# Prompt attention: turns under the single-pass type, and low-key products of two query tiles in the array's row halves

## Chip, cores and metric

One core of one Trainium2 chip. The metric is the device time of one execution in microseconds (us), as a median of several runs; lower is better. A difference of 0.2% is about what a measurement of this kernel can tell from none.

## The reference, cut to what matters

Two layers over a prompt of 2,048 tokens and 8 running streams of 16 new tokens each, in float32: first a gated short convolution, then stick-breaking attention with 16 heads of 64. The change lies wholly in the attention of the prompt:

```python
z = jnp.einsum('bqhd,bkhd->bhqk', q, k, preferred_element_type=jnp.float32) * scale
causal = kpos[None, :] < qpos[:, None]
log_keep = jnp.where(causal, jax.nn.log_sigmoid(-z), 0.0)
rev = lax.cumsum(log_keep, axis=log_keep.ndim - 1, reverse=True)
...
a = jnp.exp(log_a)
o = jnp.einsum('bhqk,bkhd->bqhd', a, v.astype(jnp.float32))
```

So each query has a weight for each earlier key: the sigmoid of their score, times the product over all keys between them of one minus their sigmoids.

## The kernel before

The kernel runs in stages: input norm and the first layer's projections, the convolution, its output projection, the values and keys, the prompt's attention (the stage of the change), and a last stage with the samples' attention and the output projection.

**Split numbers.** A float32 operand of a product is held as a high part, rounded to the type float32r (F32R), and a low part, the rest. A product of two such operands is done as several matmuls in F32R.

**The stage's work.** For each of 16 heads (eight pairs `pr`, two heads `hh` each) the 2,048 by 2,048 scores are cut into units of 512 queries by 512 keys, and each unit into four pieces of 128 queries (`q` 0 to 3). On the diagonal the pieces are 128, 256, 384 and 512 keys wide. There are 640 pieces in all, 448 of them 512 wide. Each piece goes this way:

1. TensorE, `score`: two matmuls into a buffer `pz` in PSUM, of which there are two (`ZS`). The stationary operand is the query tile in `q2`, whose 128 rows are the 64 of the high part and the 64 of the low one. The moving operand is first `kh2` (high keys, both row halves alike), L1801, then `kl2` (low keys, both halves alike), L1802.
2. ScalarE: two sigmoids of `pz`, into `a` (L1875) and, of the negated score, into `keep` (L1876). Then `pz` is free again.
3. VectorE, `scan`: the running product of `keep` from the right, into `prod` (L1926 on the diagonal, L1932 elsewhere, where it starts from the piece four before it).
4. GpSimd, `weigh`: `a` times `prod` (L1981).
5. When a unit's pieces are weighted, TensorE, `turn`: four blocks of 128 keys are turned (transposed), each with up to four instructions of 128 by 128 (L1825, 2,176 in all), into `pt`. The tile of `a` is the stationary operand, the identity the moving one, both float32.
6. ScalarE copies the block to its high part `ath` (L1885), and VectorE takes the low part `atl` as the difference (L1942).
7. TensorE, `product`: two matmuls with the values, of `ath` (L1814) and `atl` (L1816), which add up in `po`. ScalarE copies `po` out at the end of a group (L1891).

Between these, TensorE also does 280 times two parts ("chunks") of the projections for queries and gate (L1843 to L1845), whose operands SyncE loads; ScalarE (L1898, L1901) and VectorE (L1949, L1953) take up the results.

**Order.** Each engine works through a list that the class `Line` draws up when the kernel is built. It steps through time with a cost for each item (`pe_time`, `act_time`, `dve_time`, `pool_time`, and 0.1085 us for a turn of 128 columns) and takes on each engine, among the next items of each kind that could start earliest, the one with the best rank. On the chip an engine executes its list in order and waits at semaphores. SyncE's list holds the loads: the queries and keys of a head are fetched when the scores of the head two before it are done, the chunks' operands when their buffers come free.

Of the kernel before, what the change touches and what calls it, by code (L numbers as in the profile page):

```python
# [13 lines left out]
P = 128  # L14
# [1163 lines left out]

NPAIR = H // 2

ZS, TS, US, KS, PS, AS = 2, 3, 4, 4, 8, 4

Q_PAIRS = NPAIR - 2
PARTS = 4
# [6 lines left out]
X_AT = 12 * SEQ  # L1191
X_SIZE = 2 * 2 * (KT // 2) * PW * 4
LATE_SIZE = X_AT + X_SIZE + 3 * PW * 4


def is_diagonal(u):
# [51 lines left out]

ENGINES = "PE", "ACT", "DVE", "POOL", "SP"
N_HEAD, N_OUT = 2 * NPAIR, 2 * NPAIR * NGQ  # L1250
SCORE_LEAD, CHUNKS_END, CHUNKS_FROM, CHUNK_PACE = 13, 0.96, -0.01, 6


def pe_time(w):

    return w / 2400 + 0.0155


def act_time(w):
# [20 lines left out]
class Line:  # L1280


    def __init__(self):
        self.at = {}
        self.free = dict.fromkeys(ENGINES, 0.0)
        self.lines = {e: [] for e in ENGINES}
        self.loads = []
        self.pieces = [(h, n) for h in range(N_HEAD) for n in range(N_PIECE)]
        self.blocks = [(h, b) for h in range(N_HEAD) for b in range(N_BLOCK)]
        self.outs = [(h, b) for h, b in self.blocks if ends_group(b)]  # L1290
        self.chunks = all_chunks()
        self.gates = [c for c in self.chunks if c[3] == PARTS - 1]
        self.splits = [(un, m, half) for un in range(N_UN) for m in (Q, Z) for half in range(2) if (un, m) != (0, Q)]
        self.splits.sort(key=lambda s: (s[0], s[1]))
        self.next = collections.Counter()
        self.whole = sum(2 * pe_time(piece_width(n)) for _, n in self.pieces)
        self.whole += sum((QG - block_from(b) // P) * 0.1085 + 2 * pe_time(QG * P - block_from(b))
                          for _, b in self.blocks)
        self.spent = 0.0
        for part in range(PARTS):  # L1300
            self.at["x", 0, 0, part] = X_LANDS[part]
        for half in range(2):
            self.at["split", 0, Q, half] = 0.0
        for h in range(2):
            for what in KEYS:
                self.at[what, h] = 0.0 if h == 0 else FIRST_DONE
            self.at["v_in", h] = V_LANDS if h == 0 else FIRST_DONE
        for m in (Q, Z):
            self.at["raw", 0, m] = 0.0
        self.free["SP"], self.moved = X_LANDS[0] + 10.0, FIRST_DONE  # L1310
# [97 lines left out]
    def work(self, what):  # L1408

        k = self.next[what]  # L1410
        if what in ("score", "sigmoid", "scan", "weigh"):
            w = piece_width(self.pieces[k][1])
            if what == "score":
                return 2 * pe_time(w), 0.249 + 0.000469 * w - pe_time(w)
            if what == "sigmoid":
                return 2 * act_time(w), 0.185 - 0.000036 * w
            if what == "scan":
                return 0.06 + 0.0022 * w - (0.04 if w == P * QG and is_diagonal(PIECES[self.pieces[k][1]][0]) else 0), 0.135
            return pool_time(w), 0.09
        if what in ("turn", "high", "low", "product"):  # L1420
            w = QG * P - block_from(self.blocks[k][1])
            if what == "turn":
                return 0.1085 * w / P, 0.2
            if what == "high":
                return act_time(w), 0.185 - 0.000036 * w
            if what == "low":
                return dve_time(w), 0.15
            return 2 * pe_time(w), 0.249 + 0.000469 * w - pe_time(w)
# [15 lines left out]
    def place(self, engine, what, start):  # L1444
# [18 lines left out]
        if what in ("score", "sigmoid", "scan", "weigh"):  # L1463
            h, n = self.pieces[k]
            line.append((what, *divmod(h, 2), n))
            if what == "score" and n == N_PIECE - 1:
                pr, hh = divmod(h, 2)
                if pr + 1 < NPAIR:
# [53 lines left out]
    def queries(self, h):  # L1522

        pr = h // 2 + 1
        if ("scored", h) in self.at and (pr < 2 or ("made", pr) in self.at):
            ready = max(self.at["scored", h], self.at.get(("made", pr), 0.0))
            self.move(ready, 2, ("queries", *divmod(h, 2), 0), 2, 1.05, ("queries", h + 2))

    def work_of(self, what, k):

# [64 lines left out]
def phase_attend(nc, x_d, qz_v, w_room, qh_t, ql_t, kh_t, kl_t, sz_t, v_prompt, ident, oa_t, ob_t,  # L1595
# [4 lines left out]
    with ExitStack() as ctx:  # L1600
# [2 lines left out]
        at_late = lambda n, at: late(f"a_{n}1", [P, SEQ], F32R, at)  # L1603
        q2, kh2, kl2 = ([mine, at_late(n, i * 4 * SEQ)]
                        for i, (n, mine) in enumerate((("q", early.q), ("kh", early.kh), ("kl", early.kl))))
        v2 = [at_top("a_v0", [P, QT, 2, HD], F32R, V_AT), sb("a_v1", [P, QT, 2, HD], F32R)]
        x = late("a_x", [P, PARTS, PART_KT, 2, PW], F32R, X_AT)
        raw, (wh0,), (wl0,), (_, gain) = w_room
        wh, wl = [wh0, sb("a_wh1", [P, KT, P], F32R)], [wl0, sb("a_wl1", [P, KT, P], F32R)]
        v_in = sb("a_v_in", [P, 2, QT, HD])  # L1610
        a = sb("a_a", [P, US, QG, Z_W])
        keep = sb("a_keep", [P, KS, Z_W + 1])
        prod = sb("a_prod", [P, PS, Z_W + 2])
        ath = sb("a_ath", [P, AS, QG * P], F32R)
# [8 lines left out]
        restart = pb("a_restart", [P, Z_W])  # L1623
        assert nc.sbuf_base <= early.top - (TOP_SIZE - EARLY_SIZE)
        passed, passed_sp, q_rest = sem("a_passed"), sem("a_passed_sp"), sem("a_q_rest")
        qk_loaded, v_loaded = sem2("a_qk_loaded"), sem2("a_v_loaded")
        v_hi, v_ready = sem2("a_v_hi"), sem2("a_v_ready")
        z_ready, z_used, scanned, weighted = (sem("a_" + n) for n in ("z_ready", "z_used", "scanned", "weighted"))
        t_ready, at_hi, at_split, av_done = (sem("a_" + n) for n in ("t_ready", "at_hi", "at_split", "av_done"))
        ends_set, restart_set, o_read = sem("a_ends_set"), sem("a_restart_set"), sem("a_o_read")  # L1630
        x_loaded = sem2("a_x_loaded", PARTS)
        raw_loaded = sem2("a_raw_loaded")
        w_scaled, w_hi, w_ready = ([sem(f"a_w_{n}_{m}") for m in "qz"] for n in ("scaled", "hi", "ready"))
# [25 lines left out]
        def _(sp):  # L1659
            def load(pr, hh, sources):  # L1660

                rows = bass.ds((2 * pr + hh) * HD, HD)
                for dst, top, bottom in sources:
                    for part, src in ((slice(0, HD), top), (slice(HD, P), bottom)):
                        sp.dma_start(dst[hh][part, :].bitcast(F32), src[rows, 0:SEQ]).then_inc(qk_loaded[hh], 16)

            def load_v(pr, hh):
                cols = bass.ds((2 * pr + hh) * HD, HD)
# [94 lines left out]
                    load_raw(pr + 1)  # L1763

            queries, high_keys, low_keys = ((q2, qh_t, ql_t),), ((kh2, kh_t, kh_t),), ((kl2, kl_t, kl_t),)
            sp.wait_ge(early.x_stored, 16 * 4 * KT)
            load_x(0, 0)
            last_stores(sp)
# [14 lines left out]
        def _(pe):  # L1783
# [3 lines left out]
            def score(pr, hh, n):  # L1787
# [3 lines left out]
                if is_pair(pr, 0) and hh == 0:  # L1791
                    if n == 0:
                        pe.wait_ge(early.first_loaded, 96)
                    elif g == ORDER[1] and is_diagonal(u) and q == 0:
                        pe.wait_ge(q_rest, 32)
                elif n == 0:
                    pe.wait_ge(qk_loaded[hh], 96 * (pr + hh))
                pe.wait_ge(z_used, piece(pr, hh, n - ZS) + 1 + ZS)
                o = pz[:, n % ZS, 0:w]
                lhs = q2[hh][:, i * P:(i + 1) * P]  # L1800
                pe.matmul(o, lhs, kh2[hh][:, p0:p0 + w], start=True, stop=False)  # L1801
                pe.matmul(o, lhs, kl2[hh][:, p0:p0 + w], start=False, stop=True).then_inc(z_ready, 1)  # L1802

            def multiply(pr, hh, b):
                u, j = BLOCKS[b]
# [12 lines left out]

            def turn(pr, hh, b):
                u, j = BLOCKS[b]  # L1820
                if j == 0:
                    pe.wait_ge(weighted, piece(pr, hh, QG * u + QG) + N_PIECE)
                wait_past(pe, at_split, blk(pr, hh, b) + 1 - TS)
                for q in range(block_from(b) // P, QG):
                    mm = pe.transpose(pt[:, turn_slot(pr, hh, b), q * P:(q + 1) * P],  # L1825
                                      a[:, unit_slot(hh, u), q, j * P:(j + 1) * P], ident[:, :])
                mm.then_inc(t_ready, 1)

            def chunk(pr, gx, m, part):
# [87 lines left out]
        def _(dve):  # L1917
            dve.sem_inc(scanned, N_PIECE)

            def score(pr, hh, n):  # L1920
                u, q = PIECES[n]
                w, s = piece_width(n), n % PS
                dve.wait_ge(z_used, piece(pr, hh, n) + 1 + ZS)
                dve.wait_ge(weighted, piece(pr, hh, n - PS) + 1 + N_PIECE)
                if is_diagonal(u):
                    dve.tensor_tensor_scan(prod[:, s, scan_from(n):Z_W + 1][:, ::-1], keep[:, n % KS, 0:w][:, ::-1],  # L1926
                                           restart[:, Z_W - w:Z_W][:, ::-1], 0.0,
                                           ALU.mult, ALU.add).then_inc(scanned, 1)
                else:
                    dve.wait_ge(scanned, piece(pr, hh, n - QG) + 1 + N_PIECE)  # L1930
                    before = scan_from(n - QG)
                    dve.tensor_tensor_scan(prod[:, s, 0:w + 1][:, ::-1], keep[:, n % KS, 0:w + 1][:, ::-1],  # L1932
                                           restart[:, 0:1].broadcast_to([P, w + 1]),
                                           prod[:, (n - QG) % PS, before:before + 1],
                                           ALU.mult, ALU.bypass).then_inc(scanned, 1)

            def value(pr, hh, b):
# [24 lines left out]

            dve.memset(restart[:, 0:Z_W - P], 0.0).then_inc(restart_set, 1)
            dve.tensor_copy(restart[:, Z_W - P:Z_W], ident[:, :]).then_inc(restart_set, 1)
            dve.memset(keep[:, :, Z_W:Z_W + 1], 1.0).then_inc(ends_set, 1)
            dve.memset(prod[:, :, Z_W + 1:Z_W + 2], 0.0).then_inc(ends_set, 1)
            dve.wait_ge(ends_set, 2)
# [5 lines left out]
        def _(pool):  # L1973
            pool.sem_inc(weighted, N_PIECE)

            def score(pr, hh, n):
# [1 line left out]
                w, after = piece_width(n), scan_from(n) + 1  # L1978
                part = a[:, unit_slot(hh, u), q, 0:w]
                pool.wait_ge(scanned, piece(pr, hh, n) + 1 + N_PIECE)  # L1980
                pool.tensor_tensor(part, part, prod[:, n % PS, after:after + w], ALU.mult).then_inc(weighted, 1)  # L1981

            def split_v(pr, hh):

# [692 lines left out]
```

## Time and profile before

| | |
|---|---|
| median of 3 runs | 2858.61 us (2857.3 to 2861.83) |
| profiled execution, from first to last instruction | 2862.5 us |
| TensorE busy in it | 2813.8 us, 98% |
| VectorE busy | 1649.9 us, 58% |
| ScalarE busy | 1317.5 us, 46% |
| GpSimd busy | 1155.7 us, 40% |
| mean granted TensorE clock | 0.992 |

The profile shows one execution. PE is TensorE's matmuls, PEld its weight loads, DVE VectorE, ACT ScalarE, POOL GpSimd, SP SyncE. A row of a timeline has the start and the duration in us, the engine, the line of the kernel, what is written and what is read, and how many instructions it merges. The durations of matmuls overlap, since they are pipelined: what one of them costs is the time from its predecessor's end (start plus duration) to its own.

### The profile page before, as it was taken

How to read it: one execution, taken by the hardware profiler on the slowest of the kernel's cores; microseconds unless marked ns; L12 is line 12 of the kernel's file. 1: busy time of each engine (PE TensorE's matmuls, PEld its weight loads, DVE VectorE, ACT ScalarE, POOL GpSimd, SP SyncE). 2: the span in 40 equal slices, each digit the busy share in tenths (PEclk: the TensorE clock that was granted, in tenths of full speed). 3: DMA queues.
4: the chain of work that ended last, by engine and by line, in shares of the span. 5: the costliest groups of instructions: out<-in, count | busy, mean ns of one | idle time of the engine just before them, and what ended most of it. 6: DMA issues, size and time to landing. Idle time of an engine off the chain costs nothing. (4 is left out here: it accounts for less than half of the span.)

```text
span 2862.5 us, 42044 instructions
## 1 busy us (share of the span) xinstructions
PE 2813.8 (98%) x14856; PEld 2467.1 (86%) x14856; DVE 1649.9 (58%) x2151; ACT 1317.5 (46%) x2733; POOL 1155.7 (40%) x1023
## 2 busy tenths in 40 slices
PE   7999999999999999999999999999999999999998
PEld 6999999999988888889978888888888888878886
DVE  5322132213243350112268999999999999988775
ACT  6000000000043331111157888888888888875542
POOL 3333333333110120002256867676777768651110
PEclk9999999999999999999999999999999999999999
DMA  5101111111064343434687766867767776767873
GB/s 157 38 23 37 38 38 30 32 41 38 13 200 130 122 167 143 169 120 147 186 245 211 228 197 200 243 198 215 220 203 211 237 198 196 218 187 211 238 219 108
DMA packets 280359, 433.33 MB, mean 151 GB/s; under 512 B 52578, under 2 KB 218594, under 8 KB 274180
## 3 DMA queue, kind: packets, MB, share of 16 engines
q1 hardware_dynamic: 269156, 391.41, 45.1%
q0 software_dynamic: 11040, 39.86, 4.7%
q8 instruction: 89, 1.46, 0.2%
q14 instruction: 74, 0.61, 0.1%
HBM read 307.40 MB, written 123.81 MB: 151 GB/s over the span
## 5 line engine op out<-in xcount | busy, mean ns | idle before, releaser
L1981 POOL TENSOR_TENSOR a_a<-a_a,a_prod 128x512 f32<-128x512 f32 (+3 forms) x640 | 661.6, 1049 | 305.3 <-DVE a_prod L1932 183.8
L1932 DVE TENSOR_TENSOR_SCAN a_prod<-a_keep,a_prod,a_restart 128x513 f32<-128x513 f32 x384 | 476.0, 1268 | 30.2 <-ACT a_keep L1876 28.9
L1875 ACT ACTIVATE a_a<-a_pz 128x512 f32<-128x512 f32 (+3 forms) x640 | 358.0, 559 | 58.2 <-PE a_pz L1802 51.6
L1885 ACT ACTIVATE a_ath<-a_pt 128x512 fp32r<-128x512 f32 (+3 forms) x640 | 327.3, 556 | 102.2 <-PE a_po L1816 72.7
L1942 DVE TENSOR_TENSOR a_atl<-a_pt,a_ath 128x512 fp32r<-128x512 f32 (+3 forms) x640 | 359.9, 597 | 18.5 <-ACT a_ath L1885 16.1
L1876 ACT ACTIVATE a_keep<-a_pz 128x512 f32<-128x512 f32 (+3 forms) x640 | 361.6, 566 | 0.0
L1825 PE MATMUL a_pt<-ident,a_a 128*128 128x128 f32 x2176 | 316.9, 275 | 4.5 <-DVE a_atl L1942 2.4
L1825 PEld LDWEIGHTS a_pt<-ident,a_a 128*128 128x128 f32 x2176 | 262.2, 142 | 44.4 <-DVE a_atl L1942 5.0
L1801 PE MATMUL a_pz<-a_kh,a_q 128*128 128x512 f32 (+3 forms) x640 | 255.9, 403 | 3.5 <-ACTq L1866 2.0
L279 POOL TENSOR_TENSOR w_wh<-w_raw,w_gain 128x1024 fp32r<-128x1024 f32 x22 | 41.5, 1889 | 537.0 <-PE v_pg L349 279.9
L1814 PE MATMUL a_po<-a_ath,a_v 128*128 128x512 f32 (+3 forms) x640 | 245.9, 388 | 1.6 <-POOL a_v L1992 0.9
L1802 PE MATMUL a_pz<-a_kl,a_q 128*128 128x512 f32 (+3 forms) x640 | 233.8, 368 | 0.0
L347 PE MATMUL c_pg<-a_xh,c_wh 128*128 128x384 f32 (+1 forms) x640 | 231.4, 362 | 0.3 <-ACT c_cgate L496 0.3
L347 PE MATMUL c_pg<-a_xh,w_wh 128*128 128x384 f32 (+1 forms) x640 | 231.2, 361 | 0.1
L348 PE MATMUL c_pg<-a_xl,c_wh 128*128 128x384 f32 (+1 forms) x640 | 231.1, 361 | 0.0
L349 PE MATMUL c_pg<-a_xh,c_wl 128*128 128x384 f32 (+1 forms) x640 | 231.0, 361 | 0.0
L348 PE MATMUL c_pg<-a_xl,w_wh 128*128 128x384 f32 (+1 forms) x640 | 230.3, 360 | 0.0
L349 PE MATMUL c_pg<-a_xh,w_wl 128*128 128x384 f32 (+1 forms) x640 | 228.9, 358 | 0.0
L1816 PE MATMUL a_po<-a_atl,a_v 128*128 128x512 f32 (+3 forms) x640 | 227.1, 366 | 0.0
L1926 DVE TENSOR_TENSOR_SCAN a_prod<-a_keep,a_restart 128x128 f32<-128x128 f32 (+3 forms) x256 | 203.9, 813 | 27.3 <-ACT a_keep L1876 23.7
L531 DVE TENSOR_TENSOR c_u<-c_pg,c_cgate 128x512 f32<-128x512 f32 (+2 forms) x40 | 23.4, 585 | 319.5 <-PE c_pg L349 319.5
L500 ACT ACTIVATE c_sz<-c_pg 128x384 f32<-128x384 f32 (+1 forms) x40 | 21.4, 536 | 357.4 <-PE c_pg L349 357.4
(233 smaller groups left out, 6165.1 us busy)
## 6 DMA issues: line engine op xcount, KB each, us to landing
a_x<-x_d SPq DMA_DIRECT2D x84, 896.0 KB, 5.7
a_x<-x_d SPq DMA_DIRECT2D x56, 832.0 KB, 4.9
a_kh<-kh_t SPq DMA_DIRECT2D x32, 512.0 KB, 7.0
a_kl<-kl_t SPq DMA_DIRECT2D x32, 512.0 KB, 9.1
w_raw<-in_a_w_in POOLq DMA_DIRECT2D x30, 512.0 KB, 4.8
x<-f_xn POOLq DMA_DIRECT2D x17, 512.0 KB, 5.3
g_y_in<-sz_t SPq DMA_DIRECT2D x17, 512.0 KB, 7.4
g_x<-x SPq DMA_DIRECT2D x17, 512.0 KB, 3.7
```

The lines of the kernel that those rows point to most:

```text
L347: pe.matmul(out, w_h[:, kt, :], x_h[:, kt, r], start=(kt == 0), stop=False)
L348: pe.matmul(out, w_h[:, kt, :], x_l[:, kt, r], start=False, stop=False)
L349: mm = pe.matmul(out, w_l[:, kt, :], x_h[:, kt, r], start=False, stop=(kt == KT - 1))
L1801: pe.matmul(o, lhs, kh2[hh][:, p0:p0 + w], start=True, stop=False)
L1814: pe.matmul(o, v2[hh][:, kb, :, :], ath[:, b % AS, c0:], start=first, stop=False, skip_group_check=True)
L1825: mm = pe.transpose(pt[:, turn_slot(pr, hh, b), q * P:(q + 1) * P], a[:, unit_slot(hh, u), q, j * P:(j + 1) * P], ident[:, :])
L1875: act.activation(a[:, s, q, 0:w], pz[:, n % ZS, 0:w], ACT.Sigmoid, scale=SCALE)
L1876: act.activation(keep[:, n % KS, 0:w], pz[:, n % ZS, 0:w], ACT.Sigmoid, scale=-SCALE).then_inc(z_used, 1)
L1885: act.activation(ath[:, b % AS, c0:], pt[:, turn_slot(pr, hh, b), c0:], ACT.Copy).then_inc(at_hi, 1)
L1932: dve.tensor_tensor_scan(prod[:, s, 0:w + 1][:, ::-1], keep[:, n % KS, 0:w + 1][:, ::-1], restart[:, 0:1].broadcast_to([P, w + 1]), prod[: ...
L1942: dve.tensor_tensor(atl[:, b % AS, c0:], pt[:, turn_slot(pr, hh, b), c0:], ath[:, b % AS, c0:].bitcast(F32), ALU.subtract).then_inc(at_spl ...
L1981: pool.tensor_tensor(part, part, prod[:, n % PS, after:after + w], ALU.mult).then_inc(weighted, 1)
```

## The change

- **Turns.** The tile of `a` is read through a second name for the same memory, `a_bits`, with the type F32R; the identity is held in F32R too, and the output is written as F32R. Their number stays.
- **Low-key products.** Instead of the 128-row matmul of a query tile's high and low parts with the low keys, there is one of the high part alone, over 64 rows. That of the even query tile (`q` 0 or 2) reads its rows in the one row half of the array, that of the odd tile (`q` 1 or 3) in the other half, and both are issued after the odd tile's high-key matmul, one behind the other. The product of low queries and low keys is left out.
- **Signals.** Score 0 or 2 is thus reported ready only together with score 1 or 3.
- **Loads.** The odd query tiles' high part is loaded once more, into the other half (`qx`, 256 KB for a head), in the same item of SyncE's list as the queries. For the first head this load stands first in the stage's queue, and the first score waits for it. For the second head of a pair, the halves of `q2` change places.
- **Buffers and order.** `prod` has six buffers in place of eight. A scan waits for the scan two before it. `Line` counts a turn at 0.068 us, and one matmul time at an even piece and two at an odd one, in place of two at each.

```diff
-ZS, TS, US, KS, PS, AS = 2, 3, 4, 4, 8, 4
+ZS, TS, US, KS, PS, AS = 2, 3, 4, 4, 6, 4
+def half_of(hh):
+    return slice(hh * HD, (hh + 1) * HD)
...
+TURN = 0.068
...
+def score_time(n):
+    return pe_time(piece_width(n)) * (2 if n % 2 else 1)
...
         if what in ("score", "sigmoid", "scan", "weigh"):
             h, n = self.pieces[k]
             line.append((what, *divmod(h, 2), n))
+            if what == "score" and n % 2 == 0:
+                return
+            if what == "score":
+                at[what, k - 1] = end
...
+        qx = sb("a_qx", [P, QT // 2, P], F32R)
+        a_at = (nc.sbuf_base + 31) // 32 * 32
         a = sb("a_a", [P, US, QG, Z_W])
+        a_bits = nc.alloc_sbuf_tensor_at("a_bits", [P, US, QG, Z_W], F32R, offset=a_at)
+        ident_r = sb("a_ident", [P, P], F32R)
...
-                for dst, top, bottom in sources:
-                    for part, src in ((slice(0, HD), top), (slice(HD, P), bottom)):
+                for dst, first, second in sources:
+                    for part, src in ((half_of(hh), first), (half_of(1 - hh), second)):
                         sp.dma_start(dst[hh][part, :].bitcast(F32), src[rows, 0:SEQ]).then_inc(qk_loaded[hh], 16)
+                    if dst is q2:
+                        load_odd(2 * pr + hh, qk_loaded[hh])
+            def load_odd(h, loaded):
+                odd = qh_t[bass.ds(h * HD, HD), 0:SEQ].rearrange("d (i two p) -> d i two p", two=2, p=P)[:, :, 1, :]
+                sp.dma_start(qx[half_of(1 - h % 2), :, :].bitcast(F32), odd).then_inc(loaded, 16)
...
+            load_odd(0, odd_loaded)
             sp.wait_ge(early.x_stored, 16 * 4 * KT)
             load_x(0, 0)
...
                     if n == 0:
                         pe.wait_ge(early.first_loaded, 96)
+                        pe.wait_ge(odd_loaded, 16)
...
                 pe.matmul(o, lhs, kh2[hh][:, p0:p0 + w], start=True, stop=False)
-                pe.matmul(o, lhs, kl2[hh][:, p0:p0 + w], start=False, stop=True).then_inc(z_ready, 1)
+                if q % 2:
+                    even, odd = half_of(hh), half_of(1 - hh)
+                    w0 = piece_width(n - 1)
+                    pe.matmul(pz[:, (n - 1) % ZS, 0:w0], q2[hh][even, (i - 1) * P:i * P], kl2[hh][even, p0:p0 + w0],
+                              start=False, stop=True).then_inc(z_ready, 1)
+                    pe.matmul(o, qx[odd, i // 2, :], kl2[hh][odd, p0:p0 + w],
+                              start=False, stop=True).then_inc(z_ready, 1)
...
-                    mm = pe.transpose(pt[:, turn_slot(pr, hh, b), q * P:(q + 1) * P],
-                                      a[:, unit_slot(hh, u), q, j * P:(j + 1) * P], ident[:, :])
+                    mm = pe.transpose(pt[:, turn_slot(pr, hh, b), q * P:(q + 1) * P].bitcast(F32R),
+                                      a_bits[:, unit_slot(hh, u), q, j * P:(j + 1) * P], ident_r[:, :])
...
-                w, s = piece_width(n), n % PS
+                w, s = piece_width(n), piece(pr, hh, n) % PS
...
+                dve.wait_ge(scanned, piece(pr, hh, n - 2) + 1 + N_PIECE)
...
-                    dve.wait_ge(scanned, piece(pr, hh, n - QG) + 1 + N_PIECE)
...
+            dve.tensor_copy(ident_r[:, :], ident[:, :]).then_inc(ident_set, 1)
```

## Rows read from the trace of the kernel before

**Rows 1.** The page: the span in 40 slices, TensorE and VectorE busy tenths.

```profile
PE   7999999999999999999999999999999999999998
DVE  5322132213243350112268999999999999988775
```

**Rows 2.** Busy time in stretches of the stage: PE, PEld, DVE, ACT, POOL, clock, DMA.

```profile
1454.00:1490.00 36.00, 31.63 (x129) 24.21 (x129) 25.91 (x30) 23.43 (x52) 29.14 (x28) 0.83 1.05 266
1490.00:2540.00 1050.00, 1049.79 (x6148) 932.67 (x6147) 978.37 (x1283) 880.51 (x1954) 745.27 (x707) 1.00 0.72 213
2540.00:2569.00 29.00, 25.23 (x142) 20.07 (x140) 25.97 (x39) 21.90 (x51) 14.97 (x16) 0.94 0.75 217
sum 1115.00, PE 1106.65 PEld 976.95 DVE 1030.25 ACT 925.84 POOL 789.39; mean PE 368.88 PEld 325.65 DVE 343.42 ACT 308.61 POOL 263.13
```

**Rows 3.** The waits within 1454 to 2569: total us, times, longest.

```profile
ACT a_ath L1885 <- PE a_po L1816: 72.7, 100, 1.5
ACT a_a L1875 <- PE a_pz L1802: 51.6, 90, 3.4
DVE a_prod L1932 <- ACT a_keep L1876: 28.9, 58, 2.9
DVE a_prod L1926 <- ACT a_keep L1876: 23.7, 52, 1.3
DVE a_atl L1942 <- ACT a_ath L1885: 16.1, 42, 1.1
```

**Rows 4.** Groups by line, shapes kept apart: busy us, mean ns, idle before.

```profile
L1825 PE MATMUL a_pt<-ident,a_a 128*128 128x128 f32 x2176 | 316.9, 275 | 4.5 <-DVE a_atl L1942 2.4 <-POOL a_a L1981 2.1
L1802 PE MATMUL a_pz<-a_kl,a_q 128*128 128x512 f32 x448 | 177.8, 397 | 0.0
```

**Rows 5.** Timeline of TensorE's matmuls: start, duration, name, count.

```profile
2001.63 0.48 PE L1801 MATMUL a_pz<-a_kh,a_q 128*128 128x512 f32 x1
2001.94 0.39 PE L1802 MATMUL a_pz<-a_kl,a_q 128*128 128x512 f32 x1
2002.17 0.22 PE L1801 MATMUL a_pz<-a_kh,a_q 128*128 128x128 f32 x1
2002.23 0.28 PE L1802 MATMUL a_pz<-a_kl,a_q 128*128 128x128 f32 x1
2002.35 1.06 PE L1825 MATMUL a_pt<-ident,a_a 128*128 128x128 f32 x8
```

**Rows 6.** Timeline of the weight loads around the same turns.

```profile
2001.60 0.19 PEld L1801 LDWEIGHTS a_pz<-a_kh,a_q 128*128 128x128 f32 x1
2001.71 0.19 PEld L1802 LDWEIGHTS a_pz<-a_kl,a_q 128*128 128x128 f32 x1
...
2002.31 0.20 PEld L1825 LDWEIGHTS a_pt<-ident,a_a 128*128 128x128 f32 x2
```

**Rows 7.** Timeline of VectorE in a full stretch.

```profile
2104.24 1.06 DVE L1942 TENSOR_TENSOR a_atl<-a_pt,a_ath 128x384 fp32r<-128x384 f32 x3
2105.22 3.64 DVE L1932 TENSOR_TENSOR_SCAN a_prod<-a_keep,a_prod,a_restart 128x513 f32<-128x513 f32 x3
2108.77 0.67 DVE L1942 TENSOR_TENSOR a_atl<-a_pt,a_ath 128x512 fp32r<-128x512 f32 x1
```

**Rows 8.** Timeline of ScalarE: the two sigmoids of one piece.

```profile
2000.85 0.63 ACT L1875 ACTIVATE a_a<-a_pz 128x512 f32<-128x512 f32 x1
2001.33 0.64 ACT L1876 ACTIVATE a_keep<-a_pz 128x512 f32<-128x512 f32 x1
```

**Rows 9.** Timelines of SyncE's queue and TensorE where the stage begins.

```profile
1453.14 0.32 SPq L1674 DMA_DIRECT2D a_x<-x_d  x1
...
1453.63 0.32 PE L1801 MATMUL a_pz<-a_kh,a_q 128*128 128x128 f32 x1 [2.04 <-ACTq L1866]
```

**Rows 10.** DMA issues by tile: count, KB each, median us to landing.

```profile
a_q<-qh_t SPq DMA_DIRECT2D x15, 512.0 KB, 7.1
...
out<-v_rows SPq DMA_DIRECT2D x32, 256.0 KB, 2.4
```

More of the change, by code:

```diff
@@ L1295, in __init__ @@
         self.next = collections.Counter()
-        self.whole = sum(2 * pe_time(piece_width(n)) for _, n in self.pieces)
-        self.whole += sum((QG - block_from(b) // P) * 0.1085 + 2 * pe_time(QG * P - block_from(b))
+        self.whole = sum(score_time(n) for _, n in self.pieces)
+        self.whole += sum((QG - block_from(b) // P) * TURN + 2 * pe_time(QG * P - block_from(b))
                           for _, b in self.blocks)
@@ L1413, in work @@
             if what == "score":
-                return 2 * pe_time(w), 0.249 + 0.000469 * w - pe_time(w)
+                return score_time(self.pieces[k][1]), 0.249 + 0.000469 * w - pe_time(w)
             if what == "sigmoid":
@@ L1422, in work @@
             if what == "turn":
-                return 0.1085 * w / P, 0.2
+                return TURN * w / P, 0.2
             if what == "high":
@@ L1526, in queries @@
             ready = max(self.at["scored", h], self.at.get(("made", pr), 0.0))
-            self.move(ready, 2, ("queries", *divmod(h, 2), 0), 2, 1.05, ("queries", h + 2))
+            self.move(ready, 2, ("queries", *divmod(h, 2), 0), 3, 1.31, ("queries", h + 2))
     def work_of(self, what, k):
@@ L1625, in phase_attend @@
         passed, passed_sp, q_rest = sem("a_passed"), sem("a_passed_sp"), sem("a_q_rest")
+        odd_loaded = sem("a_odd_loaded")
         qk_loaded, v_loaded = sem2("a_qk_loaded"), sem2("a_v_loaded")
@@ L1630, in phase_attend @@
         ends_set, restart_set, o_read = sem("a_ends_set"), sem("a_restart_set"), sem("a_o_read")
+        ident_set = sem("a_ident_set")
         x_loaded = sem2("a_x_loaded", PARTS)
@@ L1796, in score @@
                 elif n == 0:
-                    pe.wait_ge(qk_loaded[hh], 96 * (pr + hh))
+                    pe.wait_ge(qk_loaded[hh], 112 * (pr + hh))
                 pe.wait_ge(z_used, piece(pr, hh, n - ZS) + 1 + ZS)
@@ L1820, in turn @@
                 u, j = BLOCKS[b]
+                if is_pair(pr, 0) and (hh, b) == (0, 0):
+                    pe.wait_ge(ident_set, 1)
                 if j == 0:
@@ L1933, in score @@
                                            restart[:, 0:1].broadcast_to([P, w + 1]),
-                                           prod[:, (n - QG) % PS, before:before + 1],
+                                           prod[:, (piece(pr, hh, n) - QG) % PS, before:before + 1],
                                            ALU.mult, ALU.bypass).then_inc(scanned, 1)
@@ L1980, in score @@
                 pool.wait_ge(scanned, piece(pr, hh, n) + 1 + N_PIECE)
-                pool.tensor_tensor(part, part, prod[:, n % PS, after:after + w], ALU.mult).then_inc(weighted, 1)
+                pool.tensor_tensor(part, part, prod[:, piece(pr, hh, n) % PS, after:after + w], ALU.mult).then_inc(weighted, 1)
             def split_v(pr, hh):
```

## Prediction

> **What bounds the kernel now.** I read the page's slices first, to find the stage [rows 1]: TensorE is at nine tenths nearly throughout, so its work is the span, and only in slices 21 to 36 does VectorE reach nine tenths too. That is the prompt's attention, 1454 to 2569 us. Everything that the diff touches lies in it.
>
> Then the busy times in its stretches [rows 2]. In the 1050 us of the middle TensorE is busy 1049.8 us: it is the limit. But VectorE is busy 978.4 us of them, 93%, ScalarE 880.5 (84%), GpSimd 745.3 (71%). Over the whole stage of 1115 us TensorE has 1106.7 us of work and VectorE 1030.3. The reader is to see here that whatever TensorE is spared, the stage can't fall below VectorE's 1030 us: the gap to it is 85 us, of which 10.1 stand in the first 36 us, 3.0 in the last 29, and 71.6 in the middle.
>
> The waits say the same from the other side [rows 3]: ScalarE waits for TensorE's products 72.7 us and for its scores 51.6, VectorE for ScalarE's sigmoids 28.9 and 23.7 and for its high parts 16.1. VectorE's idle time comes at second hand from TensorE.
>
> **The turns.** 2,176 instructions [rows 4]. Eight in a row end 2003.41 - 2002.51 = 0.90 us after their predecessor [rows 5], 0.11 us each, 239 us in all. The identity goes to float32r, of which the same rows have two matmuls with 128 columns, and they disagree. The first ends 0.06 us after the 512-wide one before it (2002.39 - 2002.33); the second, right behind it, takes 0.12. What differs is the weight load: the long matmul hides it, the short one doesn't. Two float32r loads start 0.11 us apart, two loads of today's turns 0.06 apart [rows 6]. So the question is which of the two the load of a float32r turn is. If the fast load belongs to the turning, a turn falls to about 0.06; if it belongs to the type float32, a turn stays at 0.11 to 0.12. The bounds are 2,176 x 0.05 = 109 us saved and 2,176 x 0.01 = 22 us lost. No row shows a float32r turn. I take 0.065, near the fast end, 98 us saved, because it is the kind of instruction and not the size that the two load rows differ in with the same 128 columns of four bytes each; I hold that for 60% likely.
>
> The Trainium skill (TensorE: Matmul & The Clock Gate, LDWEIGHTS) puts a weight load at its columns over 1.2 GHz, 0.107 us for 128, by which no turn could be under that; the trace agrees for float32r and disagrees for today's turns. By that rule this term would be 6 us instead of 98.
>
> **The low-key products.** A 512-wide one takes 2002.33 - 2002.11 = 0.22 us, a 128-wide one 0.12 [rows 5]; I interpolate 0.11 (256) and 0.17 (384) from 0.06 and 0.22, which have their loads hidden. There are 448 of 512 [rows 4] and 64 of each other width: 98.6 + 64 x 0.40 = 124 us. Afterwards there are 320 pairs. If the two of a pair run at the same time in the two halves, a pair takes the time of its wider one: 256 x 0.22 + 64 x 0.11 = 63 us, 61 saved. If the second load isn't hidden, 0.11 us comes on each pair, 35 us in all, and 26 are saved. If they run one after the other, nothing is. No row shows half-array matmuls, so a loss is possible too: if the array must empty before and after a pair, it costs a matmul's duration less its spacing, 0.39 - 0.22 = 0.17 us, twice for each of 320 pairs, 109 us, a net loss of 48. I take the full 61: the high-key matmul before a pair lasts 0.22 us, which covers two loads 0.11 apart.
>
> **TensorE after.** 1106.7 - 98 - 61 = 948 us, 85% of the stage. It no longer bounds. If neither term gives anything it still does, at 1107.
>
> **VectorE after.** Its scans and differences are the same in number and size. In a full stretch it runs without a gap: three scans of 513 columns take 3.55 us, 1.18 each [rows 7]. One copy of the identity is nothing against 1030 us. The wait for the scan two before costs nothing, since a scan always stands between. With six `prod` buffers VectorE may be six pieces ahead of GpSimd, at 1050/640 = 1.6 us each some 10 us; GpSimd has 29% to spare, so I cost this at nothing; a stall would need GpSimd to fall 10 us behind.
>
> **The paired signal.** New is that ScalarE sees two scores at once and TensorE gets both buffers back only after four sigmoids. A sigmoid takes 2001.33 - 2000.85 = 0.48 us [rows 8], four 1.92. Then follow the odd high-key product (0.22), the low pair (0.22) and the time from a matmul's end at the array to its recorded end (0.17) and ScalarE's start (taken as 0.1, an estimate): a round of 2.63 us. VectorE needs for a full pair two scans and two differences, 2 x 1.18 + 2 x 0.58 (from 4 x 1.18 to the difference at 2108.77, and 0.67 less an overlap of 0.09) = 3.5 us. So TensorE may come 0.9 us late in each round before this bounds. ScalarE fills the hole of 0.7 us with its two high parts (0.96). I leave VectorE 20 us of the 71.6 idle in the middle for what doesn't fit: bounds 0 and 71.6.
>
> **Loads.** The odd tiles come to 256 KB for each head, 4 MB over a stage that moves 213 GB/s [rows 2]: hidden, as the fetch is issued a head ahead (some 70 us). Not hidden is the first: it is issued where the stage's first load is, at 1453.14, and the first score now starts at 1453.63 [rows 9]. A 512 KB load of queries lands after 7.1 us, a 256 KB store after 2.4 [rows 10]: 1.9 to 6.6 us later, on the path, as every engine of the stage waits for scores. I take 4.
>
> **Sum.** Stage: 1030.3 + 13.1 (idle at both ends) + 20 + 4 = 1067 us in place of 1115, 48 less. Profiled execution: 2862.5 - 48 = 2814.5. The median of the runs lies 3.9 us under the profiled execution: 2810.6, rounded 2810 us, 1.7% faster.
>
> **Rivals.**
> *Turns gain nothing* (the load of float32r decides). TensorE has 1107 - 61 = 1046 us, VectorE 1030: both near full, and each pays for the other's gaps. With 30 us of mutual waits and the 4 of the first load the stage is 1080, the time 2824. For it: the only float32r loads in the trace are slow. Against: today's turns are fast with the same bytes. 20%.
>
> *The pair's round becomes the chain.* TensorE executes in order, and a chunk's six matmuls or a block's turns may stand between ScalarE's signal and the next high-key product. Over 0.9 us of lateness in each round bounds the stage; each further 0.15 us costs 48 us in 320 rounds, the whole gain. For it: ScalarE already waits 51.6 us for scores. Against: `Line` puts scores ahead when they are near due, and `keep` has four buffers. 2835 to 2865 us. 13%.
>
> *The array empties at each change between full and half rows: slower.* 109 us on TensorE, as worked out, against 61 + 98. With the turns' gain TensorE is at 1107 + 48 - 98 = 1057, and the time some 2832. Without it TensorE is at 1155: with its idle 8.3 and 4 the stage is 1167, the time 2911. It decides where the two changes of a pair cost more than 0.19 us together while the turns give nothing; with the turns' gain from about 0.5 us. Against it: turns in float32 between products in float32r show no such loss. 9%.
>
> The Trainium skill states the drain (TensorEngine Tiling (Array Packing), Tiling Modes): changing the tiling mode drains TensorE. No run here shows it yet; by it the low-key term is -48 instead of +61.
>
> *Neither edit does what it says*: turns at 0.11, low products one after the other. Only the first load's 4 us are left: 2862. 8%.
>
> **Chances and range.** Forecast (VectorE bounds) 50%, by itself 2792 to 2828. Lowest is no idle in the middle at all, 1043 us of stage: 2787. Upward the range takes in the second case and most of the third, and leaves the last two out: 2786 to 2856. A measurement tells about 0.2% from no change. Faster by over 0.2%: 50 + 20 + 7 of the third + 3 of the fourth, 80%; within: 3 of the third and half of the last, 7%; slower: 13%.
>
> **What would show it.** Turns: eight in a row under 0.6 us, and their loads 0.06 apart. Pairs: the two half-array matmuls with nearly one start, and the next matmul ending 0.22 us after them, not 0.39. VectorE busy over 96% in the middle with TensorE near 90%; ScalarE's wait for the low products of L1802's place not above 100 us. The first score 2 to 7 us after the stage's first load. The prediction is wrong if VectorE stays under 94% busy, or if TensorE's clock falls as it now idles: today 1.00 in the middle, so at 2.4 GHz, and 0.83 after the gap at the stage's start [rows 2].

## The result, and the profile after

The changed kernel takes 2996.8 us (median; 2984.7 to 3002.8), the kernel before beside it 2860.2: a ratio of 1.047 (95% interval 1.0446 to 1.0494). It is 137 us slower, where 50 us faster had been forecast. The profiled execution spans 3001.3 us.

The page's slices of the changed kernel, TensorE, VectorE and TensorE's granted clock, against [rows 1]:

```profile
PE   7999999999999999999899999999999999988998
DVE  5322123221434601022588888888888878887774
...
PEclk9999999999999999999899999999999999989999
```

The stage now runs from 1457 to 2709 us. Its stretches (columns as in [rows 2]):

```profile
1457.00:1490.00 33.00, 28.77 (x102) 19.50 (x103) 20.96 (x24) 18.58 (x40) 22.37 (x20) 0.65 1.03 268
1490.00:2680.00 1190.00, 1131.81 (x6200) 867.74 (x6199) 997.15 (x1296) 895.93 (x1970) 753.53 (x714) 0.97 0.66 194
2680.00:2709.00 29.00, 24.48 (x118) 17.51 (x116) 21.75 (x32) 18.57 (x45) 12.58 (x14) 0.79 0.41 113
sum 1252.00, PE 1185.06 PEld 904.75 DVE 1039.86 ACT 933.08 POOL 788.48; mean PE 395.02 PEld 301.58 DVE 346.62 ACT 311.03 POOL 262.83
```

In the middle TensorE is busy 95%, not the forecast 85 to 90, and not full either: 58 us of the 1190 pass without it. VectorE is busy 84%, down from 93. TensorE is still the fullest engine, but none is busy throughout. The stage has grown from 1115 to 1252 us. TensorE's busy time has risen from 1107 to 1185 us, part of it at the lower clock. The waits, against [rows 3]:

```profile
ACT a_a L1912 <- PE a_pz L1836: 197.4, 204, 6.4
...
DVE a_prod L1969 <- ACT a_keep L1913: 103.2, 135, 2.9
PEld a_pz L1834 <- issue: 91.2, 295, 0.7
PEld a_pz L1830 <- ACT a_keep L1913: 62.1, 116, 1.7
DVE a_prod L1964 <- ACT a_keep L1913: 57.4, 59, 4.0
```

ScalarE waits for paired scores 197 us where it waited 52 for single ones, VectorE for the sigmoids 161 where it was 53, and TensorE's weight loads, which before hardly waited, now wait 62 us for buffers that ScalarE has not freed. New is the third row: before the first load of a pair the load side idles 91 us in all, though nothing that the profile shows holds it. What that is stands in the timeline of matmuls, changed kernel (ends are start plus duration):

```profile
2003.49 0.40 PE L1830 MATMUL a_pz<-a_kh,a_q 128*128 128x512 f32 x1
2003.82 0.50 PE L1834 MATMUL a_pz<-a_kl,a_q 64*128 64x512 f32 x1
2003.82 0.50 PE L1836 MATMUL a_pz<-a_kl,a_qx 64*128 64x512 f32 x1
2004.25 0.28 PE L1862 MATMUL a_pt<-a_ident,a_bits 128*128 128x128 f32 x1
2004.37 0.47 PE L1849 MATMUL a_po<-a_ath,a_v 128*128 128x512 f32 x1
...
2007.28 0.49 PE L1836 MATMUL a_pz<-a_kl,a_qx 64*128 64x512 f32 x1
2007.70 0.97 PE L1862 MATMUL a_pt<-a_ident,a_bits 128*128 128x128 f32 x9
```

The weight loads of the same high-key matmul and pair:

```profile
2003.29 0.19 PEld L1830 LDWEIGHTS a_pz<-a_kh,a_q 128*128 128x128 f32 x1
2003.82 0.18 PEld L1834 LDWEIGHTS a_pz<-a_kl,a_q 64*128 64x128 f32 x1 [0.34 <-issue]
2003.82 0.18 PEld L1836 LDWEIGHTS a_pz<-a_kl,a_qx 64*128 64x128 f32 x1
```

Here the overlap breaks. Between full-array matmuls a load starts while the matmul before still runs ([rows 6]: the low-key load at 2001.71, under a matmul that ends at 2002.11). The pair's loads start at 2003.82, 0.07 us before the high-key matmul's recorded end of 2003.89, and not earlier. That is so at every one of the 320 pairs, and again for the first full-array load behind a pair (2004.25, the pair ending at 2004.32).

A low-key pair starts within 0.01 us and ends together: the two halves do run side by side. But it ends 4.32 - 3.89 = 0.43 us after the high-key matmul, and 512 columns are worth 0.23: 0.20 are lost on the way in. And the turn behind it ends 4.53 - 4.32 = 0.21 us later, where a turn after a full-array matmul takes 0.06: 0.15 more on the way out. The product behind that turn ends 4.84 - 4.53 = 0.31 us after it, 0.08 more than its width is worth. Nine turns in a row end 2008.67 - 2007.77 = 0.90 us after the pair; less the first's 0.21, eight take 0.69, 0.086 each. Their weight loads, from the timeline of loads, are nine in 0.83 us; less the last one's own 0.14 that is eight times 0.086 again:

```profile
2007.70 0.83 PEld L1862 LDWEIGHTS a_pt<-a_ident,a_bits 128*128 128x128 f32 x9 [0.24 <-issue]
```

The stage's start, SyncE's queue and the first score, against [rows 9]:

```profile
1453.39 0.65 SPq L1692 DMA_DIRECT2D a_qx<-qh_t  x1
...
1457.44 0.76 PE L1830 MATMUL a_pz<-a_kh,a_q 128*128 128x128 f32 x2 [5.59 <-DMA a_qx<-qh_t]
```

The first score starts 4.05 us after the load of the odd tiles is issued.

### The profile page after: what moved, and what is told of

Read it like the earlier page. It is cut to its first block and busy times, and to the rows that moved or that the text cites. A ratio compares the mean times of both kernels' runs of the same rounds, so it can differ in the third digit from the quotient of the medians.

```text
span 3001.3 us, 42062 instructions
## 1 busy us (share of the span) xinstructions
PE 2889.6 (96%) x14856; PEld 2392.3 (80%) x14856; DVE 1661.9 (55%) x2152; ACT 1324.4 (44%) x2733; POOL 1156.9 (39%) x1023
## 5 line engine op out<-in xcount | busy, mean ns | idle before, releaser
L1969 DVE TENSOR_TENSOR_SCAN a_prod<-a_keep,a_prod,a_restart 128x513 f32<-128x513 f32 x384 | 482.7, 1274 | 105.2 <-ACT a_keep L1913 103.2
L1912 ACT ACTIVATE a_a<-a_pz 128x512 f32<-128x512 f32 (+3 forms) x640 | 349.3, 546 | 252.9 <-PE a_pz L1836 197.4
L1979 DVE TENSOR_TENSOR a_atl<-a_pt,a_ath 128x512 fp32r<-128x512 f32 (+3 forms) x640 | 359.1, 597 | 29.8 <-ACT a_ath L1922 28.6
L1913 ACT ACTIVATE a_keep<-a_pz 128x512 f32<-128x512 f32 (+3 forms) x640 | 352.9, 551 | 0.0
L1862 PEld LDWEIGHTS a_pt<-a_ident,a_bits 128*128 128x128 f32 x2176 | 222.7, 143 | 95.5 <-DVE a_atl L1979 43.3
L1862 PE MATMUL a_pt<-a_ident,a_bits 128*128 128x128 f32 x2176 | 257.0, 254 | 29.9 <-DVE a_atl L1979 28.9
L1849 PE MATMUL a_po<-a_ath,a_v 128*128 128x512 f32 (+3 forms) x640 | 268.0, 421 | 2.5 <-ACT a_o L1928 1.3
L1851 PE MATMUL a_po<-a_atl,a_v 128*128 128x512 f32 (+3 forms) x640 | 236.8, 377 | 0.0
L1830 PEld LDWEIGHTS a_pz<-a_kh,a_q 128*128 128x128 f32 x640 | 124.9, 195 | 81.6 <-ACT a_keep L1913 62.1
```

The source lines that it names most:

```text
L1849: pe.matmul(o, v2[hh][:, kb, :, :], ath[:, b % AS, c0:], start=first, stop=False, skip_group_check=True)
L1912: act.activation(a[:, s, q, 0:w], pz[:, n % ZS, 0:w], ACT.Sigmoid, scale=SCALE)
L1913: act.activation(keep[:, n % KS, 0:w], pz[:, n % ZS, 0:w], ACT.Sigmoid, scale=-SCALE).then_inc(z_used, 1)
L1979: dve.tensor_tensor(atl[:, b % AS, c0:], pt[:, turn_slot(pr, hh, b), c0:], ath[:, b % AS, c0:].bitcast(F32), ALU.subtract).then_inc(at_spl ...
```

## The experiments

Three theories. **A, emptying**: each change between full and half rows costs TensorE, since it lets its matmuls run out first. **B, paired signal**: two scores reported together starve ScalarE and hold both score buffers, whatever the matmuls cost. **C, order**: the lists are drawn for a faster TensorE than there is. Differences below are to the kernel before timed beside each (2859.4 us for e1 to e4, 2861.7 for e5 to e8, 2861.5 for e9 to e11, 2860.2 for e12).

**e1, the turns alone** (on the kernel before):

```diff
+TURN = 0.068
-                    mm = pe.transpose(pt[...], a[...], ident[:, :])
+                    mm = pe.transpose(pt[...].bitcast(F32R), a_bits[...], ident_r[:, :])
```

> Only the float32r turns, none of the low-key pairs, eight prod buffers as before. In the trace of the changed kernel a turn behind a turn takes 0.085 us and the product after the last one 0.07 more than its width, so four turns cost 0.386 instead of 0.44 us. Theory A (all that was lost comes from the pairs of half-array matmuls): TensorE is spared some 28 us, the stage shortens, 2828 to 2845 us. Rival (the float32r turns themselves cost something, by the clock or by the order drawn with 0.068 for each): 2855 us or more.

2828.3 us, -31.1 (0.9894, 0.9878 to 0.9911). The turns gain about what their measured cost gives, 28 us, and nothing of it is lost again. The middle of its stage:

```profile
1490.00:2505.00 1015.00, 1009.64 (x6137) 891.91 (x6135) 969.98 (x1282) 877.86 (x1951) 743.57 (x707) 1.00 0.74 222
```

VectorE is busy 970 of 1015 us, 95.6%, TensorE still 99.5%.

**e2, the pairs alone** (the changed kernel with float32 turns, `TURN = 0.1085`):

> Only the pairs of half-array low-key matmuls, with turns in float32 again and counted at 0.1085. Theory A (the array empties at each change between full and half rows, 0.20 us each, 640 times, 128 us, against 61 spared): TensorE has 67 us more to do, and the time is 2925 us or more, above the changed kernel's 2997 by the turns' share if that is independent: near 3010. Theory B (the paired signal starves ScalarE): slower too, so this run alone doesn't part the two; e3 does.

2946.7 us, +87.3 (1.0316, 1.0298 to 1.0334). There is a loss in the pairs. It is some 60 us less than the 3010 expected, so the two edits don't add: 87 - 31 is 56, and the changed kernel has 137. (e10, below, has 62: with the turn's constant put right they nearly add.)

**e3, paired signal with full-array products** (on e2):

```diff
-                    pe.matmul(pz[:, (n - 1) % ZS, 0:w0], q2[hh][even, (i - 1) * P:i * P], kl2[hh][even, ...], ...)
-                    pe.matmul(o, qx[odd, i // 2, :], kl2[hh][odd, p0:p0 + w], ...)
+                    pe.matmul(pz[:, (n - 1) % ZS, 0:w0], q2[hh][:, (i - 1) * P:i * P], kl2[hh][:, ...], ...)
+                    pe.matmul(o, lhs, kl2[hh][:, p0:p0 + w], ...)
```

> As e2, with the two low-key products of a pair as full-array matmuls of 128 rows again, one behind the other after the odd tile's high-key product, still reported together; TensorE's work is that of the kernel before, and the extra loads, the first score's wait and six prod buffers stay. The order is drawn with three matmul times at the odd piece. Theory A (emptying): 2860 to 2885 us. Theory B (the paired signal makes the chain, whatever the matmuls cost): 2930 us or more.

2883.3 us, +23.9 (1.0083, 1.0066 to 1.0100). It lies in theory A's range, but TensorE's work is that of the kernel before, so theory A has no reason for the 24 us.

**e7, the rest alone** (on e2: full-array low-key product at every piece, reported by itself; extra loads, first wait and six `prod` buffers kept):

> The kernel before with nothing but the rest of the change: the odd tiles' extra loads, the first score's wait for them, six prod buffers, the scan's wait for the scan two before. Low-key products are full-array ones at each piece, each reported by itself. Expected 2862 to 2867, 4 us by the first score's wait; the other 20 us of e3's loss (2883.3) are then the paired signal's. If it is 2875 or more, the buffers or the loads are what costs, and not the signal.

2864.3 us, +2.6 (1.0012, 1.0002 to 1.0021), as expected. So of e3's 24 us the loads have 3 and the paired signal, with the order drawn for it, 21. ScalarE's wait for scores, 1490 to 2520 us, in e7 and then in e3:

```profile
ACT a_a L1896 <- PE a_pz L1823: 42.6, 80, 3.4
```

```profile
ACT a_a L1906 <- PE a_pz L1830: 115.0, 147, 1.9
```

The paired signal alone takes it from 43 to 115 us.

**e5, pairs with the order drawn for their real cost** (on e2):

```diff
-    return pe_time(piece_width(n)) * (2 if n % 2 else 1)
+    return pe_time(piece_width(n)) * (2 if n % 2 else 1) + (0.4 if n % 2 else 0.0)
```

> The pairs alone, with float32 turns, as e2 (2946.7), but the order drawn with 0.40 us more at each odd piece. If the order drawn for too fast a TensorE costs time wherever it is wrong (theory C), this gains on e2 by some 15 us or more; if what hurt the changed kernel was above all the turns counted at 0.068 on top, it stays within 6 us of e2. TensorE's surplus of some 55 us stays in both.

2936.7 us, +75.0 (1.0264, 1.0245 to 1.0283), 12 less than e2, between the two bounds stated, so that it decides for neither. Over e3, half-array pairs cost 51 us.

**e6, both in one half** (on e5; `qx` isn't read):

```diff
-                    pe.matmul(o, qx[odd, i // 2, :], kl2[hh][odd, p0:p0 + w], ...)
+                    pe.matmul(o, q2[hh][even, i * P:(i + 1) * P], kl2[hh][even, p0:p0 + w], ...)
```

> As e5, but the odd tile's low-key product reads the same row half of the array as the even tile's, so that both are half-array matmuls that can't run side by side; the order is drawn with one matmul time more at each odd piece. If side by side was worth what was reckoned, 61 us of TensorE, this comes 50 to 70 us after e5. If the two halves had gained nothing, it equals e5.

2999.2 us, +137.5 (1.0485, 1.0466 to 1.0504), 62.5 after e5. Its matmuls:

```profile
2000.10 0.40 PE L1826 MATMUL a_pz<-a_kh,a_q 128*128 128x512 f32 x1
2000.43 0.44 PE L1830 MATMUL a_pz<-a_kl,a_q 64*128 64x384 f32 x1
2000.71 0.39 PE L1832 MATMUL a_pz<-a_kl,a_q 64*128 64x512 f32 x1
2001.03 1.53 PE L1856 MATMUL a_pt<-ident,a_a 128*128 128x128 f32 x12
```

The second half-array matmul now ends 0.23 us after the first (2001.10 - 2000.87), as on the full array; the way in still costs 0.20 (0.37 for 384 columns, worth 0.17), the way out 0.15. The loads tell what it is that costs:

```profile
2000.42 0.18 PEld L1830 LDWEIGHTS a_pz<-a_kl,a_q 64*128 64x128 f32 x1 [0.33 <-issue]
2000.53 0.19 PEld L1832 LDWEIGHTS a_pz<-a_kl,a_q 64*128 64x128 f32 x1
```

The second load goes to the very half that is at work, and starts at 2000.53 under the first matmul, which ends at 2000.87. So it isn't the half rows that keep a load out, but the change from full to half. Side by side is worth what was reckoned, 61 us. And e6 differs from e3 in its two half-array products for two full ones, which take the same time, and in the 0.40 us of the order: the changes of rows cost 137.5 - 23.9 = 114 us, 320 pairs at 0.36. That is what the timeline gave, 0.20 + 0.15 to 0.20.

**e4, e10, e11, the order's costs in the changed kernel**: 0.097 for a turn (e10), 0.40 us more at an odd piece (e11), both (e4).

> The changed kernel, with the order drawn from what its trace shows: 0.097 us for a turn and 0.40 us more at each odd piece. Theory C (TensorE's extra work is only some 40 us, and the other 100 us of the loss are waits because the lists were drawn for a faster TensorE): 2900 to 2930 us. Theories A and B: within 20 us of the changed kernel's 2997.

> The changed kernel with only the turn's cost in the order put right, 0.097 for 0.068. If it is this cost whose error makes the 65 us between the changed kernel and e4, it comes near 2932; if it is the odd piece's, it stays near 2997.

> The changed kernel with only the odd piece's cost in the order put right, 0.40 us more, and a turn at 0.068. The counterpart of e10: near 2932 if this is the cost that matters, near 2997 if not; near 2960 for both if each has its half.

e4: 2932.0 (+72.6; 1.0256, 1.0239 to 1.0273), 2 us above theory C's range and 65 below the changed kernel. e10: 2923.4 (+61.8; 1.0229, 1.0209 to 1.0248). e11: 2991.4 (+129.8; 1.0465, 1.0445 to 1.0485). Theory C is shown for one constant: the turn counted at 0.068 costs 75 us. Putting the odd piece's cost right, which was wrong by far more, gains 7 us alone, no more than the executions scatter, and loses 11 beside the other (e4 against e10). Waits in 1490 to 2520 us, changed kernel and then e10:

```profile
DVE a_prod L1969 <- ACT a_keep L1913: 78.7, 111, 2.1
PEld a_pz L1830 <- ACT a_keep L1913: 44.4, 85, 1.6
PEld a_pt L1862 <- DVE a_atl L1979: 28.5, 42, 1.7
```

```profile
DVE a_prod L1969 <- ACT a_keep L1913: 58.9, 83, 3.0
PEld a_pz L1830 <- ACT a_keep L1913: 19.9, 49, 1.3
PEld a_pt L1862 <- DVE a_atl L1979: 15.6, 25, 1.7
```

With the turn counted right, VectorE waits 59 instead of 79 us for the sigmoids, TensorE's weight loads 20 instead of 44 for a free score buffer and 16 instead of 29 for a free `pt`.

**e8, the same constant with the turns alone** (on e1, `TURN = 0.097`):

> The float32r turns alone, as e1 (2828.3), with a turn counted at 0.097 us in the order, which is what its trace shows, in place of 0.068. Theory C, that counting a turn too cheap costs waits: 2815 to 2825 us. Otherwise within 3 us of e1.

2828.9 us, -32.8 (0.9882, 0.9863 to 0.9902): the same as e1. Here the wrong cost did no harm.

**e9 and e12, turns under the paired signal, full-array products**, with 0.097 and with 0.068:

> The changed kernel with full-array low-key products at the paired place, a turn counted at 0.097 us and an odd piece at three matmul times: float32r turns and the paired signal, no change between full and half rows. If the turns' gain of 31 us is kept under the paired signal: 2883 - 31 = 2852. If the paired signal is by then the limit (theory B, in the place where TensorE has been relieved), the turns gain 10 us or less: 2873 or more.

> As e9 (float32r turns, paired signal, full-array low-key products, 2863.3), with a turn counted at 0.068 instead of 0.097. With the turns alone this error cost nothing (e1 against e8), in the changed kernel it cost some 70 us (e10). If the paired signal is what makes the order so sensitive, this is 2900 us or more; if it takes the half-array matmuls too, it stays under 2875.

e9: 2863.3 us, +1.8 (1.0006, 0.9996 to 1.0016). Against e3 the turns gain 22 of their 31 us, between the two cases expected. e12: 2899.0, +38.8 (1.0139, 1.0122 to 1.0156), just short of the 2900 stated for the paired signal's side: the constant costs 37 us as soon as the signal is paired, and 75 with the half-array matmuls on top.

## Why the prediction was wrong

The 137 us, by differences of the runs above (each uncertain by some 6 us, the last by some 9):

| | us | from |
|---|---|---|
| extra loads, first wait, six buffers | +3 | e7 |
| paired signal | +21 | e3 - e7 |
| changes between full and half rows | +114 | e6 - e3 |
| low-key products side by side | -63 | e5 - e6 |
| float32r turns, and e5's 0.40 us taken out of the order | -13 | e10 - e5 |
| a turn counted at 0.068 | +75 | changed kernel - e10 |

The turns' share depends on the order that each variant has: with the 0.40 us in both, the turns gain 2 us (e4 - e5), with it in neither 25 (e10 - e2), and alone 31 (e1).

Where the time stands is in the stage's own sums (from 1453 us to its end, profiled executions):

| | stage | TensorE busy | idle |
|---|---|---|---|
| before | 1116.0 | 1107.0 | 9.0 |
| e3 | 1135.3 | 1109.4 | 25.9 |
| e5 | 1190.8 | 1162.2 | 28.6 |
| e6 | 1252.4 | 1227.1 | 25.3 |
| e9 | 1115.3 | 1081.8 | 33.5 |
| e12 | 1148.8 | 1090.3 | 58.5 |
| e10 | 1174.8 | 1145.3 | 29.5 |
| changed | 1254.8 | 1184.0 | 70.8 |

The paired signal (e3) is idle time of TensorE. The changes of rows (e6 against e3) are 118 us of its busy time and no idle time: no wait for another engine explains them. The wrong constant is idle time above all (e12 against e9), and in the changed kernel half idle and half busy.

- **What bounds the kernel now**: right. TensorE was full, and VectorE's 1030 us are a floor that no variant reached: relieved of 28 us of turns, e1 comes to 95.6% of VectorE in the middle and follows TensorE almost one for one.
- **The turns**: mis-sized. Taken at 0.065 us, 98 us saved. They cost 0.085 in a run, and 0.07 to 0.08 more on the product behind it: 0.06 + 3 x 0.085 + 0.07 is 0.385 for four, 0.097 each with rounding, 28 us saved. The load was neither of the two in [rows 6]: loads of float32r turns start 0.085 us apart.
- **The low-key products**: here the prediction failed most. "I take the full 61" should have read a net loss of about 50, 112 us the other way. The step was the choice between the bounds: it argued that the high-key matmul covers the pair's two loads. It is long enough, but they don't start under it: they start 0.07 us before its recorded end, at all 320 pairs. And it let the absence of a loss between float32 and float32r speak against emptying, which is a change of type and not of rows. The rival had the mechanism and nearly the price (0.34 a pair, measured 0.36), with 9% for it. That the price came so near is partly luck: it was a matmul's duration less its spacing, twice 0.17, and the two changes measure 0.20 and 0.15 to 0.20. The Trainium skill (TensorEngine Tiling (Array Packing), Tiling Modes) says that a change of tiling mode drains TensorE; the runs agree, at 0.36 us for the two changes of a pair.
- **TensorE after**: 1107 + 51 - 28 = 1130 us at the full clock, an estimate, not 948; e10 has 1145, some of it at the lower clock. No single step turned the sign. By the prediction's own reckoning emptying alone, with 98 us saved on the turns, would still have been faster (2832). The low-key products and the turns together put TensorE 23 us above what it was; the paired signal and the order's constant, which the sum had nearly at nothing, did the rest.
- **The paired signal**: the round was reckoned with a TensorE that has 15% to spare. It had none, so each wait of TensorE for score buffers lengthened the stage: 21 us (e3). The sum had 20 us of idle time too, but of VectorE and out of a surplus that wasn't there, so that the two numbers are alike is luck. The second rival named this chain.
- **What no step held**: that the constants of the order are a change too. The prediction read 0.068 as a claim and not as an input. e10, e12 and e8 show that it costs 75, 37 and nothing. That the pairing makes the lists brittle is shown, and that TensorE then idles more; which places in the lists do it isn't. The waits of e10 fit turns placed where VectorE hasn't freed `pt` and scores placed where ScalarE hasn't freed their buffer, but that is argued. In the changed kernel a part goes through the clock: in its middle the granted clock is 0.97, so some 6% of it at 1.2 GHz, where the kernel before has 1.00 [rows 2], and the profiled execution of e10 has 0.988 over all against the changed kernel's 0.977. That is (0.023 x 3001 - 0.012 x 2921) x 2 = 68 us more at half speed, which can cost 34 us at most. The four executions of the changed kernel itself run from 3002.8 us at 0.977 to 2984.7 at 0.986, 2 us for each 0.001, which would make it some 22. The rest isn't the clock, and neither are e12's 37 us: its profiled execution has 0.992, as e9's.
- **The signs named beforehand**: two of them came, VectorE under 94% busy (84) and a falling clock (0.97), and ScalarE's wait for the low products was above 100 us (197).
- **The first load**: right, the first score starts 3.8 us later than before (1457.44 - 1453.63) against 4 forecast, with e7's 2.6 in all.
- **Six buffers, scan's wait**: right as far as e7 tells, with scores reported singly: nothing beside the first load.

The version to keep is e1: the turns without the pairs, 1.1% faster than before.

## What to carry to other kernels

Where two half-array products replace two full ones, count the changes between full and half rows first: here a pair gained 0.20 us and paid 0.36, so by these numbers at least two pairs would have to share the two changes, which no run tried. A result that is reported later than before costs even where no work is added, most of all where only two buffers stand between the engines. And where a kernel's order is drawn from a table of costs, a constant edited in it is a change with a price of its own: measure it alone.

## What the runs showed of the hardware

- Going from 128-row to 64-row matmuls cost 0.20 us, going back 0.15 before a turn and 0.20 before a 512-wide product (which ends 0.43 us after the pair and is worth 0.23), with float32 turns (e2) as with float32r ones.
- A weight load started under the running matmul where both had 128 rows or both 64 (e6, in the same half too), but at a change of rows only 0.07 us before its recorded end, at all 320 pairs of the changed kernel and of e2.
- Two 64-row matmuls in different halves start within 0.01 us of each other and take the time of one; in the same half they take the time of two.
- A turn takes 0.11 us in float32, and 0.06 in float32r behind a 512-wide product. Behind another turn a float32r one takes 0.085, the spacing of their weight loads, between the 0.06 and the 0.11 of [rows 6].
